# A block with attention and routed experts on one core: thirty-two more tokens by gathered rows, dense products on 352 columns

## The chip, the cores and the metric

One core of a Trainium2 chip runs the kernel. The metric is the device time of one execution in microseconds (us); the kernel before and the kernel after are compared by the medians of their runs.

## What is computed

The reference is one layer on 512 tokens of width 1024: a modulation vector from `c`, windowed attention and latent attention, a projection, and then a feed-forward of routed experts. The last part fills some three quarters of the time, and the change lies in it:

```python
def peer_ffn(h, w_query, sub_keys, u_table, v_table):
    q = (xt @ w_query).reshape(T, PEER_HEADS, 2, PEER_KEY_DIM // 2)
    s = jnp.einsum('thpd,hpnd->thpn', q, sub_keys)
    s_top, i_top = lax.top_k(s, K)                       # K = 16, 128 keys
    cand = (s_top[:, :, 0, :, None] + s_top[:, :, 1, None, :]).reshape(T, PEER_HEADS, K * K)
    best, bi = lax.top_k(cand, K)
    e = ...                                              # expert number, of 128 * 128
    g = jax.nn.softmax(best, axis=-1)
    a = gelu(einsum('tkd,td->tk', u_table[e], x))        # 8 heads * 16 = 128 experts a token
    y = einsum('tk,tkd->td', g * a, v_table[e])
```

Each token has 128 experts out of 16,384; `u_table` and `v_table` have 16,384 rows of 1024 floats each, 64 MB a table.

## The kernel before

The feed-forward has two ways to do the same thing. For three token blocks of 128 (384 tokens) it is dense: it computes the products with all 16,384 rows of `u`, tile by tile of 128 rows, takes the gelu, multiplies by a gate that is zero for experts that a token has not chosen, and multiplies by all of `v`. For the fourth block (128 tokens) it fetches the chosen rows: for each of the 128 slots (8 heads x 16) one indirect DMA gathers 128 rows of 4 KB, one for each token.

The first pass runs over the 128 tiles of `u` (line 1110). For tile n, SyncE loads 512 KB (`load_tile`, line 401), ScalarE rounds them to `hi` (line 723), GpSimd takes the rest `lo` (`low_u`, line 488), and TensorE does 24 matmuls of 384 columns (`dot`, lines 1085 to 1087). ScalarE's gelu (line 748) goes out to DRAM. `high(n + 2)` and so `low_u(n + 2)` wait for `dot(n - 1)`, so GpSimd is at most three tiles ahead.

Beside it VectorE searches the experts of a token block (`search`), in this order: block 0 of the search order is the gathered one (tiles 0 to 12), then three dense blocks, each with a search stretch of 18 tiles and a building stretch of 16 tiles, which begin at tiles 30, 64 and 98. In a building step, VectorE makes one-hot matrices for 8 tokens, ScalarE weighs them, and TensorE multiplies them into gates (`token_gates`, line 1096) after the dot of its tile. Gates of the first two dense blocks go to DRAM, those of the last stay in `stage`.

The rows are gathered by GpSimd in its one program order, between the `low_u` of the tiles (line 497). Five row buffers are used in turn: a gather waits until the buffer's last row was used (`row_used`), and a list written out ahead, `row_step`, holds it back to a tile. VectorE's `row_dot` (line 1443) multiplies a gathered row of `u` with the token (`x_tok`, in PSUM). There are 4 such rows in each search stretch and 2 or 3 in each building step. ScalarE's `weights(p)` is the exponential of a search; for block 0 it stands behind the gelu of tile 13. When all 128 are done (tile 115) ScalarE takes their gelu, and VectorE begins with the rows of `v` (`row_sum`, line 1543), 12 of them before the second pass.

The second pass runs over the 128 tiles of `v` (`mix`, lines 1132 to 1134, 24 matmuls of 384 columns for each tile). VectorE weighs the gelus that come back with the gates (`weigh`, lines 1521 and 1523), takes `lo` of the tile (`low_v`, line 1532) and of the weighed gelus (`low_c`, line 1527), and sums one more gathered row per tile. Sums are in y_tok, which is transposed to the output at the end (line 1150).

## Time and profile before

| | us |
|---|---|
| median of 3 runs | 1587.39 |
| lowest, highest | 1583.72, 1588.54 |
| profiled execution | 1583.69 |
| its span from first to last instruction | 1581.6 |

```profile
PE 1503.6 (95%) x8487; PEld 1392.4 (88%) x8487; DVE 1221.5 (77%) x2498; ACT 720.0 (46%) x1352; POOL 622.9 (39%) x414
```

PE is TensorE's matmuls, PEld its weight loads, DVE VectorE, ACT ScalarE, POOL GpSimd, SP SyncE. The numbers are busy time, its share of the span and instructions.

### The profile page before, as it was taken

To read this page: it belongs to the slowest core of one execution; us is meant where nothing else is said; L and a number is where in the kernel's file an instruction comes from. 1 tells how busy PE (TensorE), PEld (TensorE's weight loads), DVE (VectorE), ACT (ScalarE), POOL (GpSimd) and SP (SyncE) were. 2 spreads that over 40 slices of the span, in tenths; PEclk is the share of its full clock that TensorE was granted. 3 is DMA by queue.
4 is the path that set the end of the run, shared out by engine and by line. 5 is a ranking of instruction groups with operands and counts; after the bars stand their busy time and mean duration, and the time that the engine had idled before them with its cause. 6 is when DMAs were issued, how large, how long until landed. Compare 5 with 4: busy or idle time off the path is not lost.

```text
span 1581.6 us, 23400 instructions
## 1 busy us (share of the span) xinstructions
PE 1503.6 (95%) x8487; PEld 1392.4 (88%) x8487; DVE 1221.5 (77%) x2498; ACT 720.0 (46%) x1352; POOL 622.9 (39%) x414
## 2 busy tenths in 40 slices
PE   3898999989969999999999999999999999999998
PEld 3464566868969999999999999999999999999998
DVE  3857676865979688978899685778888888888874
ACT  1235465233323777357754777333333333333331
POOL 2001000201757777677777777932222222222200
PEclk9999579999989999999999999999999999999999
DMA  9820100443757699998999899899999999999973
GB/s 323 279 103 1 54 1 10 152 180 120 231 176 237 224 322 325 372 320 295 325 350 333 272 319 335 258 342 331 336 327 341 325 330 337 326 338 330 327 238 106
DMA packets 148369, 405.25 MB, mean 256 GB/s; under 512 B 15392, under 2 KB 49440, under 8 KB 147360
## 3 DMA queue, kind: packets, MB, share of 16 engines
q1 hardware_dynamic: 90816, 242.39, 45.5%
q0 software_dynamic: 36864, 134.23, 23.5%
q10 hardware_dynamic: 20576, 27.15, 4.7%
q8 instruction: 68, 1.11, 0.3%
q14 instruction: 45, 0.37, 0.1%
HBM read 356.53 MB, written 47.19 MB: 255 GB/s over the span
## 4 chain that ended last, share of the span: by engine, by line
PE 89%; DVE 3%; DMA 3%; ACT 2%; POOL 1%; issue 1%; SPq 0%; ACTq 0%; DVEq 0%
PE ps L1132 11%; PE ps L1134 11%; PE ps L1133 11%; PE ps L1085 10%; PE ps L1087 10%; PE ps L1086 10%; PE ps L1096 5%; PE ps L860 4%; PE ps L977 2%; PE ps L947 2%; PE ps L960 1%; PE ps L950 1%; DVE m L1178 1%; PE ps L1008 1%; DMA ring<-in_w_ada 1%
## 5 line engine op out<-in xcount | busy, mean ns | idle before, releaser
L723 ACT ACTIVATE hi<-raw 128x1024 fp32r<-128x1024 f32 x256 | 271.1, 1060 | 375.4 <-PE ps L1134 337.1
L488 POOL TENSOR_TENSOR lo<-raw,hi 128x1024 fp32r<-128x1024 f32 x128 | 327.4, 2560 | 194.0 <-ACT hi L723 190.6
L1085 PE MATMUL ps<-h2hi,hi 128*128 128x384 f32 x1024 | 347.9, 340 | 13.1 <-POOL lo L488 13.1
L1087 PE MATMUL ps<-h2hi,lo 128*128 128x384 f32 x1024 | 343.6, 336 | 0.0
L1086 PE MATMUL ps<-h2lo,hi 128*128 128x384 f32 x1024 | 343.3, 335 | 0.0
L1132 PE MATMUL ps<-chi,hi 128*128 128x384 f32 x1000 | 334.8, 335 | 3.2 <-DVE lo L1532 3.2
L1134 PE MATMUL ps<-chi,lo 128*128 128x384 f32 x1000 | 334.7, 335 | 0.0
L1133 PE MATMUL ps<-clo,hi 128*128 128x384 f32 x1000 | 334.6, 335 | 0.0
L1532 DVE TENSOR_TENSOR lo<-raw,hi 128x1024 fp32r<-128x1024 f32 x128 | 156.7, 1225 | 104.4 <-ACT hi L723 104.4
L1085 PEld LDWEIGHTS ps<-h2hi,hi 128*128 128x128 f32 x1024 | 193.2, 189 | 13.8 <-POOL lo L488 13.8
L1086 PEld LDWEIGHTS ps<-h2lo,hi 128*128 128x128 f32 x1024 | 193.2, 189 | 0.0
L1087 PEld LDWEIGHTS ps<-h2hi,lo 128*128 128x128 f32 x1024 | 192.9, 188 | 0.0
L1132 PEld LDWEIGHTS ps<-chi,hi 128*128 128x128 f32 x1000 | 188.3, 188 | 3.6 <-DVE lo L1532 3.6
L1133 PEld LDWEIGHTS ps<-clo,hi 128*128 128x128 f32 x1000 | 188.3, 188 | 0.0
L1134 PEld LDWEIGHTS ps<-chi,lo 128*128 128x128 f32 x1000 | 188.2, 188 | 0.0
L497 POOL DMA_INDIRECT rows<-in_v_tiles,E x76 | 80.5, 1059 | 219.4 <-DVE y_tok L1543 212.8
L748 ACT ACTIVATE act_out<-ps 128x384 f32<-128x384 f32 x128 | 62.3, 487 | 174.4 <-PE ps L1087 171.6
L759 ACT ACTIVATE ohW<-eqI,wS 128x128 f32<-128x128 f32 x384 | 118.2, 390 | 29.7 <-DVE eqI L1482 29.1
L1443 DVE SCALAR_TENSOR_TENSOR rows<-rows,ps 128x1024 f32<-128x1024 f32 x78 | 94.8, 1220 | 22.2 <-DMA rows<-in_u_rows,E 17.4
L1543 DVE SCALAR_TENSOR_TENSOR y_tok<-rows,cc,y_tok 128x1024 f32<-128x1024 f32 x76 | 107.0, 1407 | 4.7 <-DMA rows<-in_v_tiles,E 4.3
L1096 PE MATMUL ps<-ohW,ohJ 128*128 128x128 f32 x768 | 99.1, 278 | 5.4 <-issue 2.4
L1096 PEld LDWEIGHTS ps<-ohW,ohJ 128*128 128x128 f32 x768 | 93.1, 191 | 12.2 <-issue 7.6
(279 smaller groups left out, 2164.9 us busy)
## 6 DMA issues: line engine op xcount, KB each, us to landing
raw<-in_u_tiles SPq DMA_DIRECT2D x128, 512.0 KB
raw<-in_v_tiles SPq DMA_DIRECT2D x128, 512.0 KB
gelus<-act_out ACTq DMA_DIRECT2D x128, 192.0 KB
act_in<-gelus SPq DMA_DIRECT2D x128, 192.0 KB, 5.1
gates<-stage SPq DMA_DIRECT2D x32, 512.0 KB
gate<-gates SPq DMA_DIRECT2D x32, 512.0 KB
late<-in_w_ada SPq DMA_DIRECT2D x4, 2048.0 KB, 8.5
qkT<-in_w_ada SPq DMA_DIRECT2D x3, 2048.0 KB, 14.3
```

The source lines that it names most:

```text
L488: nc.gpsimd.tensor_tensor(lo[m % 3][:], raw[m % 3][:], hi[m % 3][:].bitcast(F32), ALU.subtract).then_inc(u_lo, 1)
L723: nc.scalar.activation(hi[m % 3][:], raw[m % 3][:], ACT.Copy).then_inc(t_hi, 1)
L759: last = nc.scalar.activation(ohW[half][:, t, :], eqI[:, half, t, :], ACT.Copy, scale=wS[:, col:col + 1])
L1085: nc.tensor.matmul(out, hi[n % 3][:, cols], h2hi[:, 0:ND, k, :], start=(k == 0), stop=False)
L1086: nc.tensor.matmul(out, hi[n % 3][:, cols], h2lo[:, 0:ND, k, :], start=False, stop=False)
L1087: last = nc.tensor.matmul(out, lo[n % 3][:, cols], h2hi[:, 0:ND, k, :], start=False, stop=(k == KD - 1))
L1096: last = nc.tensor.matmul(ps[:, 2 + half, t * P:(t + 1) * P], ohJ[half][:, t, :], ohW[half][:, t, :], start=True, stop=True)
L1132: nc.tensor.matmul(out, hi[m % 3][:, cols], chi[n % 4][:], start=(n == 0), stop=False)
L1133: nc.tensor.matmul(out, hi[m % 3][:, cols], clo[n % 4][:], start=False, stop=False)
L1134: last = nc.tensor.matmul(out, lo[m % 3][:, cols], chi[n % 4][:], start=False, stop=False)
L1532: tt_(lo[m % 3][:], raw[m % 3][:], hi[m % 3][:].bitcast(F32), ALU.subtract).then_inc(v_lo, 1)
L1543: nc.vector.scalar_tensor_tensor(out=y_tok[:], in0=row, scalar=cc[:, n:n + 1], in1=y_tok[:], op0=ALU.mult, op1=ALU.add).then_inc(row_used, 1)
```

## The change

32 tokens of the third dense block move from the dense way to the gathered one. The dense products have 352 columns instead of 384. The last building stretch has 12 steps instead of 16 and ends at tile 110 instead of 114. The 32 tokens' rows are gathered four slots at a time: one indirect DMA fetches 4 slots of each of 32 tokens, so that 32 more transfers suffice for `u` and 32 for `v`, 160 of each instead of 128.

`h2hi` and `h2lo`, the moving operand of `dot`, are laid out in groups of 32 tokens, so that 352 columns are 11 runs of 32, where 384 were 3 runs of 128. `x_tok` is made by 8 transposes at tile 4 (`turn_tokens`) from a sum that VectorE writes, instead of by 16 matmuls ahead of tile 0; at tile 111 it is made again for the 32 tokens, each four times. Their expert numbers and weights go to DRAM and back with four small DMAs on SyncE in the last building stretch. Their 32 `row_dot` follow from tile 112 on, three a tile by `row_step`; ScalarE's gelu of all the row products moves from tile 115 to tile 123, and the 12 early `row_sum` move behind it. In the second pass every sixth tile has two `row_sum`. At the end `y_more` is folded to 32 tokens by one matmul for each of 8 column groups.

In the search stretches 6 rows instead of 4 are used (1, 1, 2, 2). `weights(0)` moves from tile 13 to tile 10, and the first gather from GpSimd's tile 13 to tile 14.

```diff
-TD = ND * P
+XT = 32
+XR = P // XT
+TD = ND * P - XT
 SLOTS = PH * KTOP
+SU = SLOTS + SLOTS // XR
...
-        FILL, PER_BUILD, EARLY = 4, (2, 3), 12
+        steps_of = {p: BUILD if p < TT - 1 else BUILD - XT // (2 * HB) for p in range(1, TT)}
+        tail_at = build_at[TT - 1] + steps_of[TT - 1]
+        FILL, PER_BUILD, EARLY, MORE = (1, 1, 2, 2), (2, 3), 12, 6
...
-        row_step = row_step[:SLOTS] + [tail_at + 2 + j for j in range(EARLY)] + [NT + n for n in range(NT - EARLY)]
+        sums_at = [n for n in range(NT) for _ in range(2 if n % MORE == MORE - 1 else 1)][:SU - EARLY]
+        more_at = tail_at + 3 + (SU - SLOTS) // 3
+        row_step = row_step[:SLOTS] + [tail_at + 2 + j // 3 for j in range(SU - SLOTS)] + \
+            [more_at + 1 + j // 3 for j in range(EARLY)] + [NT + n for n in sums_at]
...
+                if m == build_at[TT - 1] + 6:
+                    sp.wait_ge(more_ready, 1)
+                    sp.dma_start(more[0], Ef[P - XT:P, :]).then_inc(more_out, 16)
+                    sp.dma_start(more[1], IJW[P - XT:P, 2, :, :].rearrange("p h k -> p (h k)")).then_inc(more_out, 16)
+                if m == build_at[TT - 1] + 8:
+                    sp.wait_ge(more_out, 32)
+                    sp.dma_start(E2[:].bitcast(F32), more[0].rearrange("t (r k) -> (t r) k", r=XR)).then_inc(more_in, 16)
+                    sp.dma_start(wg[:, SLOTS:SU], more[1].rearrange("t (r k) -> (t r) k", r=XR)).then_inc(more_in, 16)
...
-                while g < 2 * SLOTS and (row_step[g - NROWS] <= m - 3 if g >= NROWS else m >= S0 + 1):
+                while g < 2 * SU and (row_step[g - NROWS] <= m - 3 if g >= NROWS else m >= S0 + 2):
...
-                    if n == search_at[p] + (13 if p == 0 else 14):
+                    if n == search_at[p] + (10 if p == 0 else 14):
                         weights(p)
-                if n == tail_at + 1:
-                    act.wait_ge(row_used, SLOTS)
+                if n == more_at:
+                    act.wait_ge(row_used, SU)
                     nc.scalar.activation(cc[:], aa[:], ACT.Gelu).then_inc(aa_gelu, 1)
...
+            def turn_tokens(part, done):
+                pe.wait_ge(x_cols, done)
+                if done == 1:
+                    pe.wait_ge(s_copied, TT)
+                else:
+                    pe.wait_ge(row_used, SLOTS)
+                for k in range(KD):
+                    cols = slice(k * P, (k + 1) * P)
+                    last = nc.tensor.transpose(x_tok[:, cols], part[:, cols], ident[:])
+                last.then_inc(x_tok_ready, 1)
...
-                    nc.tensor.matmul(out, hi[n % 3][:, cols], h2hi[:, 0:ND, k, :], start=(k == 0), stop=False)
+                    nc.tensor.matmul(out, hi[n % 3][:, cols], dense(h2hi, k), start=(k == 0), stop=False)
...
+                if d == 0:
+                    pe.wait_ge(row_used, 2 * SU)
+                    pe.wait_ge(spread_ready, 1)
+                nc.tensor.transpose(ps[:, d, ND * P:T], y_tok[:, cols], ident[:])
+                nc.tensor.matmul(ps[:, d, TD:ND * P], y_more[:, cols], spread[:], start=True, stop=True).then_inc(y_ps, 1)
...
-                if n + EARLY < NT:
-                    row_sum(n + EARLY)
+                for j, at in enumerate(sums_at):
+                    if at == n:
+                        row_sum(EARLY + j)
```

## Rows read from the trace of the kernel before

**Rows 1.** The page's part on the chain that ended last, shares by engine.
```profile
PE 89%; DVE 3%; DMA 3%; ACT 2%; POOL 1%; issue 1%; SPq 0%; ACTq 0%; DVEq 0%
```

**Rows 2.** TensorE's waits from 400 us on: total us, times, longest us.
```profile
PE ps L1085 <- POOL lo L488: 13.1, 2, 12.9
PE ps L1132 <- DVE lo L1532: 3.2, 1, 3.2
```

**Rows 3.** Chain pieces (start, us, what): 32 matmuls of 512 columns, twice.
```profile
289.02 7.27 PE ps L1015 x32
...
344.44 7.25 PE ps L1015 x32
```

**Rows 4.** Windows: stretch, us, busy PE, PEld, DVE, ACT, POOL, PEclk, DMA, GB/s.
```profile
640.00:660.00 20.00, 20.00 (x117) 20.00 (x116) 19.72 (x89) 7.78 (x10) 13.13 (x6) 1.00 1.02 393
...
800.00:820.00 20.00, 19.62 (x117) 19.17 (x117) 19.80 (x99) 9.55 (x18) 14.52 (x10) 1.00 1.00 357
...
1040.00:1060.00 20.00, 19.72 (x105) 19.72 (x106) 15.56 (x25) 6.08 (x9) 4.58 (x4) 0.91 1.00 367
...
1200.00:1400.00 200.00, 200.00 (x1156) 200.00 (x1155) 164.83 (x242) 70.72 (x97) 49.76 (x49) 1.00 0.96 332
```

**Rows 5.** DMA queues (packets, MB, share) and issues (count, KB, us to landing).
```profile
q0 software_dynamic: 36864, 134.23, 23.5%
...
raw<-in_v_tiles SPq DMA_DIRECT2D x128, 512.0 KB
...
act_in<-gelus SPq DMA_DIRECT2D x128, 192.0 KB, 5.1
...
gate<-gates SPq DMA_DIRECT2D x32, 512.0 KB
```

**Rows 6.** Timeline 440 to 467 us (start, us, what), of DVE, POOL and PE.
```profile
449.31 0.29 DVE L1473 TENSOR_REDUCE eS<-eW 128x8 f32<-128x128 f32 x1 [8.35 <-ACT eW L770]
...
451.03 1.12 POOL L497 DMA_INDIRECT rows<-in_u_rows,E  x1 [10.13 <-DVE E L1490]
...
466.10 0.33 PE L1085 MATMUL ps<-h2hi,hi 128*128 128x384 f32 x1
```

**Rows 7.** Chain pieces in building: token gates; a loop from hi to gates.
```profile
533.18 1.78 PE ps L1096 x16
539.14 1.78 PE ps L1096 x16
...
626.99 1.78 PE ps L1096 x16
...
728.38 1.06 ACT hi L723
...
734.57 7.99 DMA rows<-in_u_rows,E
...
745.82 1.13 PE ps L1096 x8
```

**Rows 8.** Timeline of POOL in a building step with three gathers.
```profile
955.92 2.40 POOL L488 TENSOR_TENSOR lo<-raw,hi 128x1024 fp32r<-128x1024 f32 x1 [1.23 <-ACT hi L723]
...
962.13 2.41 POOL L488 TENSOR_TENSOR lo<-raw,hi 128x1024 fp32r<-128x1024 f32 x1 [0.22 <-ACT hi L723]
```

**Rows 9.** Timeline: DVE's second search begins and ends; PE turns its result.
```profile
630.41 2.80 DVE L1423 MAX8 sv<-s 128x8 f32<-128x128 f32 x14
...
694.38 0.51 DVE L1476 TENSOR_TENSOR IJW<-eW,eR 128x128 f32<-128x128 f32 x1
...
703.51 0.49 PE L1103 MATMUL ps<-ident,IJW 128*128 128x128 f32 x3
```

**Rows 10.** Timeline of DVE: a row sum beside low_u, one without.
```profile
1012.08 2.96 DVE L1543 SCALAR_TENSOR_TENSOR y_tok<-rows,cc,y_tok 128x1024 f32<-128x1024 f32 x1 [1.39 <-DMA rows<-in_v_tiles,E]
...
1056.94 1.28 DVE L1543 SCALAR_TENSOR_TENSOR y_tok<-row_hi,cc,y_tok 128x1024 f32<-128x1024 f32 x1
```

**Rows 11.** Timeline of PE: the last three tiles of the second pass begin.
```profile
1564.60 0.44 PE L1146 MATMUL ps<-chi,hi 128*128 128x384 f32 x1 [2.46 <-DVE lo L1532]
```

More of the change, by code:

```diff
@@ L163, in build @@
         (row_lo,), _ = region(at2 + (TT + ND) * KD * P * 4, [("row_lo", [P, D], F32)])
+        x_part = rows[0]
         rows = [t[:] for t in rows + [row_hi, row_lo]]
@@ L369, in group, with dense, gathered, gathered_more @@
             return (p - 1) * 2 * BUILD + 2 * i + half
-        NGROUPS = ND * 2 * BUILD
+        NGROUPS = 2 * sum(steps_of.values())
+        def dense(of, k):
+            return of[:, 0:TD // XT, k, :]
+        def gathered(of):
+            return of[:, ND * P // XT:T // XT, :, :]
+        def gathered_more(of):
+            return of[:, TD // XT, :, :].unsqueeze(3).to_broadcast([P, KD, XT, XR])
         block = ctx.enter_context(nc.Block())
@@ L1067, in _ @@
                 key_scores(tt)
-            pe.wait_ge(h2_split, KD)
             pe.wait_ge(s_copied, TT - 1)
-            pe.wait_ge(identr_ready, 1)
-            for k in range(KD):
-                out = x_tok[:, k * P:(k + 1) * P]
-                nc.tensor.matmul(out, h2hi[:, TT - 1, k, :], identr[:], start=True, stop=False)
-                last = nc.tensor.matmul(out, h2lo[:, TT - 1, k, :], identr[:], start=False, stop=True)
-            last.then_inc(x_tok_ready, 1)
+            def turn_tokens(part, done):
[8 more added lines that the diff above has]
+                last.then_inc(x_tok_ready, 1)
             def dot(n):
@@ L1084, in dot @@
                     cols = slice(k * P, (k + 1) * P)
-                    nc.tensor.matmul(out, hi[n % 3][:, cols], h2hi[:, 0:ND, k, :], start=(k == 0), stop=False)
-                    nc.tensor.matmul(out, hi[n % 3][:, cols], h2lo[:, 0:ND, k, :], start=False, stop=False)
-                    last = nc.tensor.matmul(out, lo[n % 3][:, cols], h2hi[:, 0:ND, k, :], start=False, stop=(k == KD - 1))
+                    nc.tensor.matmul(out, hi[n % 3][:, cols], dense(h2hi, k), start=(k == 0), stop=False)
+                    nc.tensor.matmul(out, hi[n % 3][:, cols], dense(h2lo, k), start=False, stop=False)
+                    last = nc.tensor.matmul(out, lo[n % 3][:, cols], dense(h2hi, k), start=False, stop=(k == KD - 1))
                 last.then_inc(a_ps, 1)
@@ L1418, in _, with top16 @@
             dve.sem_inc(ada_read, 1)
-            def top16(vals, idx, lists, n, between):
+            def top16(vals, idx, lists, n, between, fills):
                 for a in range(n):
@@ L1427, in top16 @@
                 settled(last)
-                between()
+                between(fills[0])
                 for a in range(n):
@@ L1434, in top16 @@
                 settled(last)
-                between()
+                between(fills[1])
                 for a in range(n):
@@ L1534, in row_sum @@
             def row_sum(n):
-                g = SLOTS + n
+                g = SU + n
                 dve.wait_ge(row_in[g % NROWS], 16 * (g // NROWS + 1))
                 dve.wait_ge(cc_ready, 1)
-                row = rows[g % NROWS]
-                if n == 0:
-                    nc.vector.tensor_scalar(y_tok[:], row, cc[:, n:n + 1], None, ALU.mult).then_inc(row_used, 1)
+                if n == SLOTS:
+                    dve.wait_ge(a_ps, NT)
+                row, y = rows[g % NROWS], y_tok if n < SLOTS else y_more
+                if n in (0, SLOTS):
+                    nc.vector.tensor_scalar(y[:], row, cc[:, n:n + 1], None, ALU.mult).then_inc(row_used, 1)
                 else:
                     dve.wait_ge(row_used, g)
-                    nc.vector.scalar_tensor_tensor(out=y_tok[:], in0=row, scalar=cc[:, n:n + 1], in1=y_tok[:],
+                    nc.vector.scalar_tensor_tensor(out=y[:], in0=row, scalar=cc[:, n:n + 1], in1=y[:],
                                                    op0=ALU.mult, op1=ALU.add).then_inc(row_used, 1)
+            dve.wait_ge(oh_used, NGROUPS + 2)
+            tt_(y_tok[:].rearrange("p (k t r) -> p k t r", k=KD, r=XR), gathered_more(h2hi).bitcast(F32), gathered_more(h2lo).bitcast(F32), ALU.add)\
+                .then_inc(x_cols, 1)
+            for g in range(SLOTS, SU):
+                row_dot(g)
             dve.wait_ge(aa_gelu, 1)
+            dve.wait_ge(more_in, 32)
             tt_(cc[:], cc[:], wg[:], ALU.mult).then_inc(cc_ready, 1)
```

89 lines of the change are left out of this document (54 added, 35 removed).

## Prediction

> **What bounds the kernel now.** I read the chain of work that ended last first: 89% of it is TensorE [rows 1]. Then TensorE's own waits from 400 us on, to see whether something else is nearly late: in some 1180 us they are one stop of 12.9 us behind GpSimd and one of 3.2 us at the start of the second pass, and little else [rows 2]. Then the windows of the second pass: TensorE is busy for all of 200 us, while the DMA engines are busy for 0.96 of it and move 332 GB/s [rows 4]. So the kernel is bound by matmul columns, with the transfers close behind. The change removes columns and adds transfers; all depends on what is late next.
>
> **What a tile costs.** In the second pass 1156 matmuls of 384 columns start in 200 us [rows 4], 173.0 ns each, so 24 of them take 4.15 us. 32 matmuls of 512 columns take 7.27 us, 227 ns each [rows 3]. The difference is 0.42 ns a column, one column a cycle of the full clock. 352 columns then take 159.5 ns and a tile 3.83 us, 0.32 us less. The new moving operand of `dot` comes in 11 runs of 32 columns. No row has such runs; the nearest is the second of the two pieces, whose operand `h2hi` comes in 4 runs of 128 and which takes 7.25 us, where the first, contiguous one takes 7.27 [rows 3]. I take nothing for it, and price it as a rival.
>
> I now follow the first pass from landmark to landmark, in the times of the profiled span.
>
> **Start to tile 15.** Now VectorE waits 8.35 us for the exponential behind tile 13's gelu, ending at 449.31; the expert numbers follow 1.7 us later, GpSimd stands at the first gather for 10.13 us, does five and only then the next `low_u`; `dot(15)` starts at 466.10 [rows 6]. With the exponential at tile 10 VectorE finds it done, so the numbers are ready at 442.7. GpSimd is then through `low_u(14)`. A gather takes it 1.2 us ((6.0 - 2.4) / 3) [rows 8], five 6.1, and `low_u(15)` 2.4, so `dot(15)` can start at 451.5. By columns it would be ready a little earlier: without the stop of 12.9 us it would be at 453 now, some 4 us less with shorter tiles, and the 8 transposes at tile 4 add 0.7 (three start 0.25 us ahead of the dot that follows, so 0.08 each) [rows 9]. So 451.5 is the start, 14.6 us earlier.
>
> **Tiles 15 to 30.** 15 x 3.83 = 57.5 us give 509.0. VectorE's search now begins at 443 and took 64.5 us in the second block (630.41 to 694.89) [rows 9]. Two more row products of 1.3 us make 67.1, and the first rows, which are gathered at 443 to 449, may keep it waiting: I take 70, bounds 67 and 72. TensorE waits for it, where in the second block it comes 8.6 us after (694.89 to 703.51) [rows 9]. Start of building: 513.
>
> **Building stretches.** A step costs 5.96 us when nothing waits (533.18 to 539.14), but 15 steps take 93.8 us, 6.25 each [rows 7]. The difference is a loop: after one step's gates ScalarE rounds, GpSimd subtracts and gathers, the rows land 7 to 8 us after issue, VectorE uses them and only then makes the one-hots; 728.38 to 745.82 is 17.4 us of it [rows 7], and it spans three steps. Shorter dots don't shorten this loop. The floor becomes 5.64; bounds are 5.64 and 6.25, and I take 6.05, since most stalled steps will be set by the loop as before. 16 steps: 96.8 us, twice; the last stretch has 12: 72.6.
>
> **Search stretches two and three.** 18 x 3.83 + 0.3 = 69.2 us. VectorE starts 1.6 us after the first of these dots (630.41 against 626.99 + 1.78) [rows 7, 9] and needs 64.5 + 2.6: done at 68.7. So 69.7 each, with no slack left. The small DMAs on SyncE at tiles 104 and 106 wait for things that are long done and sit ahead of loads that have two tiles of lead: nothing.
>
> Sum: 513 + 96.8 = 609.8; + 69.7 = 679.5; + 96.8 = 776.3; + 69.7 = 846.0; + 72.6 = 918.6 at the end of the building.
>
> **Tiles 110 to 127.** TensorE alone needs 18 x 3.83 + 0.7 = 69.6 us. But from GpSimd's tile 115 on there are three gathers behind each `low_u`. In a building step that had three, `low_u` to the next possible one took 6.0 us (955.92 to 962.13 less 0.22 of waiting) [rows 8]. A tile's transfers are 0.52 + 0.18 MB and three gathers of 0.524 (134.23 MB over 256) [rows 5], 2.28 MB; at 6.0 us that is 380 GB/s, about as much as the fullest window shows (393) [rows 4]. I take 6.15. `low_u(115)` ends 15.8 us into this part; ten such tiles later `low_u(125)` ends at 77.3, `low_u(127)` at 84.9, and `dot(127)` at 90.0. That is 20 us behind the columns.
>
> **The turn to the second pass.** ScalarE's gelu of the row products needs the 160th row: gathered in tile 123, used at 76. The rows of `v` that five buffers hold come along, but the other seven gathers are issued behind `low_u(127)`. A landing takes between the 5.1 us of the loads of `act_in` and the 8.0 of a gather in the building [rows 5, 7]; I take the lower, since the burst is short. With 1.2 us to issue, 1.3 a sum and five buffers, that is some 1.6 us each: the twelfth is summed at 103, and `low_v(0)` follows at 106.2, as VectorE takes it after all twelve. TensorE waits 16 us, where it now waits 3.2 [rows 2]. `low_v(0)`, and `load_tile` behind it on SyncE, wait for the same. Row sums took 2.96 us beside a `low_u` and 1.28 without one [rows 10]; only the first few fall beside it. Bounds 99 and 116. The page SBUF — State Buffer of the Trainium skill (its part on the two sides of SBUF and their shared port pair) says that a VectorE operation with two SBUF inputs and a GpSimd operation exclude each other; the 2.96 us agree. Second pass starts at 918.6 + 106.2 = 1024.8.
>
> **The second pass.** Bytes of a tile: 0.524 + 0.197 + 0.131 + 0.524 = 1.376 MB now [rows 5], which at 4.15 us are the 332 GB/s read [rows 4]. After it is 0.524 + 0.180 + 0.131 + 148/127 x 0.524 = 1.446 MB, and 3.83 us would ask for 377 GB/s. The window in which this pass catches up moved 367, and windows in the first pass 357 and 393 [rows 4]. VectorE is busy 164.83 of 200 us, 3.42 a tile, and comes to 3.56 with 0.165 sums more and 0.05 less of columns: below 3.83, and a tile with two sums (4.7) is covered by the two tiles that it is ahead. I take 3.90, a little over the columns. 125 x 3.90 = 487.5 us. The clock falls once after the wait, as it does now (0.91 over 20 us) [rows 4]: 1.7 us. Then the 2.46 us stop and the end, 17.0 us from 1564.60 [rows 11]; two more row sums lie behind the last `low_v` now and TensorE waits for them at the first column group: 2.8 us. The fold matmuls (0.1 us each) eat what the columns save there.
>
> 1024.8 + 1.7 + 487.5 + 2.5 + 2.8 + 17.0 = 1536.3 us of span against 1581.6. The profiled execution took 1583.69, 2.1 more than its span, so 1538.4; the median of the runs is 3.7 above it, so 1542.
>
> The page DMA: Bandwidth & Descriptors of the Trainium skill (part Bandwidth) gives some 358 GB/s as what HBM yields to a core, which speaks against this change; but 393 GB/s over 20 us [rows 4] is more. It is the first rival below.
>
> **Rivals.**
> 1. The transfers set the second pass. If a backlog moves no more than the 357 GB/s of 800 to 820 us, at a DMA share of 1.00 [rows 4], a tile takes 1.446 / 0.357 = 4.05 us: 19 us more, and 2 in tiles 115 to 125: 1563. For it: DMA share 0.96 already. Against: the 393. The same with the waiting in each transfer kept as it is (0.96 x 1.446/1.376 of 4.15 us): 4.18 us, 1577. The page's limit would give nearly the 4.05.
> 2. The turn is worse: row landings of 8.0 us and sums of 2.96 us [rows 7, 10], or a clock at half while TensorE idles 2.3 of each 6.15 us (a tile then takes up to 7.7): 15 to 25 us more, 1562.
> 3. Slower: a run of 32 columns costs something at each join. There are 10 joins x 24 x 128. From 2.4 ns a join (6 columns) a dot is 0.58 us longer and the gain is gone (74 plain tiles x 0.58, and 44 building tiles past the loop's slack). At 4 ns: 74 x 0.96 + 44 x 0.55 = 95 us, 1637. Against it: no cost for runs of 128 [rows 3]; for it, no row this short.
> 4. The columns don't count, since weight loads bound a matmul: tile stays 4.15, +10 to 40 us, about 1585. Against it: 512 and 384 columns differ by a cycle for each column, so at 384 the columns set the time [rows 3, 4].
>
> **How the numbers follow.** Forecast 0.47 (1522 to 1556); rival 1 0.20 at 1563 and 0.08 at 1577; rival 2 0.13; rival 4 or mixtures near no change 0.04; rival 3, with any mixture of 1 and 2 that overshoots, 0.08. The range 1522 to 1578 takes the bounds of the building step (5.75 to 6.25: -13 to +9 us), of the turn (-7 to +10) and of the second pass (3.83 to 4.16: -9 to +33). Faster by over 0.3% 0.88, within 0.3% (about what a measurement of this kernel can tell) 0.04, slower 0.08.
>
> **What would show it.** `dot(15)` near 451; plain tiles at 3.83; building steps near 6.05; `low_u` 6.1 us apart at tiles 115 to 125 with TensorE waiting for it; a stop of some 16 us ahead of line 1132's counterpart for `low_v`; second pass tiles at 3.90 with TensorE mostly busy. It is wrong if tiles of the second pass stand at 4.0 or more with ScalarE's `hi` waiting for DMA, or if plain dots are longer than their columns.

## The result and the profile after

The changed kernel takes 1571.6 us (median of 6 runs, 1570.1 to 1577.3) against 1584.8 us (6 runs). The ratio is 0.991, with a 95% interval of 0.989 to 0.993: some 13 us less. One execution each of e2_one_run and e9_half_rows took far longer than the others of its kernel (4207.9 and 2785.5 us) and is left out of the figures below. The forecast was 1542. The sign was right, and two thirds of the gain did not come. The profiled execution took 1575.6 us with a span of 1573.1; the working had 1536.3 for it, so 36.8 us of span have to be found.

The page, its part on busy time of the changed kernel:

```profile
PE 1449.0 (92%) x8439; PEld 1332.0 (85%) x8439; DVE 1265.0 (80%) x2583; ACT 706.4 (45%) x1311; POOL 768.1 (49%) x478
```

TensorE works 54.6 us less than before, and the span is only 8.5 us shorter: 46 us have become waiting. TensorE's waits from 400 us on, changed kernel (us in total, times, longest), to be held against [rows 2]:

```profile
PE ps L1123 <- POOL lo L519: 24.8, 15, 3.0
PE ps L1134 <- DVE ohJ L1531: 21.2, 9, 5.0
PE ps L1174 <- DVE lo L1588: 16.9, 1, 16.9
PE ps L1188 <- DVE lo L1588: 2.5, 1, 2.5
```

Before there was one stop of 12.9 us behind GpSimd. Now 15 tiles wait for GpSimd's low part, nine building steps wait for VectorE's one-hots, and the turn waits 16.9 us.

Windows of the changed kernel (columns as in [rows 4]): the second pass, a search stretch, and the tail of the first pass.

```profile
1100.00:1300.00 200.00, 200.00 (x1259) 200.00 (x1258) 184.75 (x273) 79.69 (x106) 103.62 (x62) 1.00 1.01 379
...
820.00:860.00 40.00, 40.00 (x245) 40.00 (x245) 39.51 (x163) 15.26 (x20) 27.76 (x14) 1.00 1.01 377
...
980.00:1000.00 20.00, 16.27 (x87) 15.38 (x86) 8.86 (x15) 6.10 (x8) 17.21 (x15) 0.91 0.94 343
1000.00:1020.00 20.00, 14.67 (x78) 13.79 (x77) 12.48 (x21) 4.57 (x6) 17.33 (x15) 0.92 1.01 389
```

In the second pass TensorE is busy throughout, 200 / 1259 = 158.9 ns a matmul (forecast 159.5), while the DMA engines move 379 GB/s. In the search stretch it is also busy throughout, but a matmul takes 40 / 245 = 163.3 ns. In the tail the DMA engines are full and TensorE is not.

Where the time stands, from the starts of the dots in the two traces and the forecast (us; a stretch is from the start of one dot to that of the other, and `mix(0)` is the start of the second pass):

| stretch | before | forecast | after |
|---|---|---|---|
| start to dot(15) | 466.1 | 451.5 | 457.8 |
| dot(15) to dot(30) | 62.6 | 61.5 | 64.0 |
| building, dot(30) to dot(46) | 99.8 | 96.8 | 105.2 |
| search, dot(46) to dot(64) | 75.2 | 69.7 | 75.4 |
| building, dot(64) to dot(80) | 100.5 | 96.8 | 106.4 |
| search, dot(80) to dot(98) | 75.2 | 69.7 | 73.2 |
| building, dot(98) to dot(110) | 74.5 | 72.6 | 77.6 |
| tail and turn, dot(110) to mix(0) | 86.3 | 106.2 | 111.3 |
| mix(0) to the end | 541.3 | 511.5 | 502.2 |

The second pass gave more than was forecast. Every stretch of the first pass is longer than forecast, and the building stretches, with fewer columns, are longer than before.

The largest single stop is in the third step of each building stretch. The chain of work through the first of them, changed kernel (start, us, what):

```profile
528.28 1.06 ACT hi L757
529.35 0.07 issue
529.41 2.41 POOL lo L519
531.83 0.14 issue
531.97 7.12 DMA rows<-in_u_rows,E
539.09 0.02 issue
539.11 1.23 DVE rows L1490 x2
540.34 0.60 DVE eqI L1529
540.94 0.61 DVE ohJ L1531
541.55 0.80 issue
542.35 3.67 PE ps L1134 x16
```

`low_u(33)` has to be done before a gather is issued at 531.97. Its row lands 7.12 us later, and only then does VectorE make the one-hots for the gates of tile 32. `dot(33)` starts 12.50 us after `dot(32)` where 5.73 is the step. At tiles 67 and 101 the pitches are 12.40 and 10.99.

### The profile page after: what moved, and what is told of

It is laid out like the page before. It is cut to its first block, busy times and chain, and to the rows that moved or that the text cites. A ratio compares the mean times of both kernels' runs of the same rounds, so it can differ in the third digit from the quotient of the medians.

```text
span 1573.1 us, 23445 instructions
## 1 busy us (share of the span) xinstructions
PE 1449.0 (92%) x8439; PEld 1332.0 (85%) x8439; DVE 1265.0 (80%) x2583; ACT 706.4 (45%) x1311; POOL 768.1 (49%) x478
## 4 chain that ended last, share of the span: by engine, by line
PE 66%; DVE 10%; POOL 9%; DMA 8%; ACT 3%; issue 3%; ACTq 0%; SPq 0%; DVEq 0%
PE ps L1174 10%; PE ps L1175 10%; PE ps L1176 10%; POOL lo L519 6%; DMA rows<-in_u_rows,E 5%; PE ps L1123 5%; PE ps L1125 4%; PE ps L1124 4%; PE ps L893 4%; PE ps L1134 2%; PE ps L1010 2%; POOL rows L531 2%; PE ps L980 2%; PE ps L993 1%; PE ps L983 1%
## 5 line engine op out<-in xcount | busy, mean ns | idle before, releaser
L1123 PE MATMUL ps<-h2hi,hi 128*128 128x352 f32 x1024 | 346.7, 339 | 25.8 <-POOL lo L519 24.8
L1125 PE MATMUL ps<-h2hi,lo 128*128 128x352 f32 x1024 | 340.1, 332 | 0.0
L1174 PE MATMUL ps<-chi,hi 128*128 128x352 f32 x1000 | 322.6, 323 | 16.9 <-DVE lo L1588 16.9
L1124 PE MATMUL ps<-h2lo,hi 128*128 128x352 f32 x1024 | 337.9, 330 | 0.0
L1175 PE MATMUL ps<-clo,hi 128*128 128x352 f32 x1000 | 322.3, 322 | 0.0
L1176 PE MATMUL ps<-chi,lo 128*128 128x352 f32 x1000 | 322.3, 322 | 0.0
L531 POOL DMA_INDIRECT rows<-in_v_tiles,E x96 | 153.3, 1597 | 151.2 <-DVE y_tok L1601 121.4
L1490 DVE SCALAR_TENSOR_TENSOR rows<-rows,ps 128x1024 f32<-128x1024 f32 x96 | 116.0, 1219 | 54.3 <-DMA rows<-in_u_rows,E 53.0
L781 ACT ACTIVATE act_out<-ps 128x352 f32<-128x352 f32 x128 | 58.9, 460 | 172.2 <-PE ps L1125 163.6
L792 ACT ACTIVATE ohW<-eqI,wS 128x128 f32<-128x128 f32 x352 | 108.2, 390 | 40.9 <-DVE eqI L1529 40.8
L1134 PE MATMUL ps<-ohW,ohJ 128*128 128x128 f32 x704 | 95.6, 289 | 24.3 <-DVE ohJ L1531 21.2
```

Source lines behind the costliest of these rows:

```text
L531: nc.gpsimd.indirect_dma_start(rows[g % NROWS], None, table, bass.IndirectOffsetOnAxis(ap=at, axis=0)).then_inc(row_in[g % NROWS], 16)
L1123: nc.tensor.matmul(out, hi[n % 3][:, cols], dense(h2hi, k), start=(k == 0), stop=False)
L1124: nc.tensor.matmul(out, hi[n % 3][:, cols], dense(h2lo, k), start=False, stop=False)
L1125: last = nc.tensor.matmul(out, lo[n % 3][:, cols], dense(h2hi, k), start=False, stop=(k == KD - 1))
L1134: last = nc.tensor.matmul(ps[:, 2 + half, t * P:(t + 1) * P], ohJ[half][:, t, :], ohW[half][:, t, :], start=True, stop=True)
L1174: nc.tensor.matmul(out, hi[m % 3][:, cols], chi[n % 4][:], start=(n == 0), stop=False)
```

## The experiments

All edits are to the changed kernel, but for `e3_exp_alone`. Six kernels compute other numbers than the reference (e2_one_run, e8_both_one_run, e9_half_rows, e10_half_rows_vector, e13_half_low_start, e14_half_low_search): they are for their times alone. Ratios are to the kernel before in the same group of runs, with their 95% interval; 0.001 is 1.6 us. The changed kernel has 0.991.

**The held gathers (e1_rows_early).**

```diff
-            row_step += [search_at[p] + 3 * (j + 1) for j in range(sum(FILL))]
+            row_step += [search_at[p] + at for at in (3, 6, 9, 11, 13, 15)]
```

> The six rows of a search stretch are given to tiles 3, 6, 9, 11, 13 and 15 of the stretch in the list that holds gathers back, instead of 3, 6, 9, 12, 15 and 18; nothing else changes. Theory A: the list holds the third row of the second building step back to GpSimd's tile build_at + 3, and that makes the stop of some 6.5 us in the third step of each building stretch (pitches 12.50, 12.40 and 10.99 us at tiles 33, 67 and 101). Then those three pitches fall to 6 to 7.5 us and the kernel is 14 to 19 us faster than the changed kernel, 1553 to 1558. Theory B: the landing of 7 us and the loop of the building steps make the stop, wherever the gather stands; it then moves to a neighbouring step, and the kernel gains less than 4 us, 1568 or more.

1552.1 us, ratio 0.979 (0.977 to 0.980): 19.5 us less than the changed kernel. All three pitches are 5.73. GpSimd's timeline at the place, e1_rows_early:

```profile
528.08 2.41 POOL L519 TENSOR_TENSOR lo<-raw,hi 128x1024 fp32r<-128x1024 f32 x1 [3.21 <-ACT hi L757]
530.63 0.95 POOL L531 DMA_INDIRECT rows<-in_u_rows,E  x1
531.89 0.94 POOL L531 DMA_INDIRECT rows<-in_u_rows,E  x1 [0.30 <-issue]
```

Two gathers stand there, where the changed kernel has three:

```profile
529.41 2.41 POOL L519 TENSOR_TENSOR lo<-raw,hi 128x1024 fp32r<-128x1024 f32 x1 [3.22 <-ACT hi L757]
531.97 0.95 POOL L531 DMA_INDIRECT rows<-in_u_rows,E  x1
533.23 0.94 POOL L531 DMA_INDIRECT rows<-in_u_rows,E  x1 [0.30 <-issue]
534.47 0.94 POOL L531 DMA_INDIRECT rows<-in_u_rows,E  x1 [0.30 <-issue]
```

The first of the three is for the fifth row of the stretch, which the second step uses. `row_step` gave the sixth search row to tile 18 of the stretch, the first of the building, so the gather five rows on was held with those of the building. The three building stretches lose 4.4, 6.4 and 3.7 us, 14.5 of the 18.0 us of span; the rest is the small balance of the start, the search stretches (one of which is 1.5 us longer) and the tail. Theory A holds, and the pitches fell further than it had them (6 to 7.5).

**The joins (e2_one_run).**

```diff
-            return of[:, 0:TD // XT, k, :]
+            return of[:].rearrange("p g k c -> p (g k c)")[:, k * TD:(k + 1) * TD]
```

> The moving operand of dot is read as one run of 352 columns from the same buffers, which holds other tokens' and other features' numbers, so the dense products of the first pass are of other data; the count of matmuls and columns is the same. Theory A: the 10 joins of each matmul cost 5.4 ns (pitch 3.95 us a plain tile in the first pass, 3.82 in the second, where the operand is one run). Then plain tiles of the first pass stand at 3.82 to 3.84 us; some 66 of them are bound by TensorE, which gives 8 us, and the building steps give 0 to 4: 1560 to 1564. Theory B: the 0.13 us a tile comes from something else that the first pass has (weights that GpSimd and ScalarE write meanwhile); the pitch stays at 3.95 and the time within 2 us of the changed kernel.

The pitches are close to theory A: plain tiles at 3.81 us (tiles 20 to 26) and 3.87 us (tiles 48 to 55 and 82 to 89) instead of 3.95, building steps at 5.60 at least instead of 5.73. So the joins cost 0.08 to 0.14 us a tile, 3.3 to 5.6 ns a matmul. The same window as above, e2_one_run:

```profile
820.00:860.00 40.00, 40.00 (x250) 40.00 (x249) 39.44 (x138) 16.17 (x22) 30.98 (x14) 1.00 0.99 372
```

In this window it is 160.0 ns a matmul instead of 163.3. The time does not follow: 1577.3 us, ratio 0.995 (0.993 to 0.997), which is above the changed kernel, though the profiled execution's span is 5.5 us shorter. TensorE waits longer for GpSimd (31.2 us against 24.8) and for the one-hots (24.3 against 21.2). So the cost of a join is shown, and its worth in the whole kernel is not: there is only the 5.5 us between two single executions, and that of the changed kernel (1575.6 us) lies 4 us above its median. Why the other runs were slower is open.

**The exponential and the first gather alone (e3_exp_alone), on the kernel before.**

```diff
-                    if n == search_at[p] + (13 if p == 0 else 14):
+                    if n == search_at[p] + (10 if p == 0 else 14):
...
-                while g < 2 * SLOTS and (row_step[g - NROWS] <= m - 3 if g >= NROWS else m >= S0 + 1):
+                while g < 2 * SLOTS and (row_step[g - NROWS] <= m - 3 if g >= NROWS else m >= S0 + 2):
```

> The kernel before with one part of the change alone: the first exponential behind the gelu of tile 10 instead of 13 and the first gather behind GpSimd's tile 14 instead of 13. Theory A (the forecast's step): the stop of 12.9 us ahead of dot 15 goes, and nothing else is late until the first building stretch, so the kernel is 10 to 13 us faster than before, 1572 to 1575. Theory B: the search of the second token block or a stop at tiles 15 to 30 takes most of it back, as in the changed kernel, where dot 30 comes only 6.9 us earlier than before: 3 to 7 us, 1578 to 1582.

1572.1 us, ratio 0.993 (0.990 to 0.996), 13.3 us less than before. TensorE's waits for GpSimd, e3_exp_alone:

```profile
PE ps L1085 <- POOL lo L488: 2.4, 2, 2.2
```

The stop of 12.9 us is gone and nothing takes its place. This two-line part alone is worth as much as the whole change.

**The other part alone (e12_tokens_alone).** Both edits of e3 taken back in the changed kernel.

```diff
-                    if n == search_at[p] + (10 if p == 0 else 14):
+                    if n == search_at[p] + (13 if p == 0 else 14):
...
-                while g < 2 * SU and (row_step[g - NROWS] <= m - 3 if g >= NROWS else m >= S0 + 2):
+                while g < 2 * SU and (row_step[g - NROWS] <= m - 3 if g >= NROWS else m >= S0 + 1):
```

> The changed kernel without the move of the first exponential and of the first gather: the exponential stands behind the gelu of tile 13 again, the first gather behind GpSimd's tile 13. So it is the 32 tokens' part of the change with the six rows a search stretch. Theory A: the parts add. The move alone gave 13.3 us (e3_exp_alone) and the whole change 13.2, so that the tokens' part gives nothing by itself: 1582 to 1588. Theory B: in the changed kernel part of the move's gain is lost again at tiles 15 to 30, so undoing it costs less, 5 to 10 us: 1576 to 1581.

1580.4 us, ratio 0.997 (0.995 to 0.999): theory B, by a little. The 32 tokens as they were written bring 2 to 8 us; the move is worth 9 us within the changed kernel. As theory B has it, part of the move's gain goes again at tiles 15 to 30, which take 64.0 us in the changed kernel and 59.4 here. Its trace again has

```profile
PE ps L1123 <- POOL lo L519: 18.5, 2, 12.9
```

from 400 to 520 us.

**The turn (e4_five_early).**

```diff
-        FILL, PER_BUILD, EARLY, MORE = (1, 1, 2, 2), (2, 3), 12, 6
+        FILL, PER_BUILD, EARLY, MORE = (1, 1, 2, 2), (2, 3), 5, 4
```

> 5 row sums instead of 12 ahead of the second pass, and two sums in every fourth tile of it instead of every sixth. Theory A: TensorE's wait of 16.9 us at the turn is for the seven gathers behind low_u(127) and their sums, so that it falls to 5 to 9 us and the kernel is 8 to 12 us faster than the changed kernel, 1560 to 1564. Theory B: the wait passes to another (the gelu of the row products, or the gelus that come back), or VectorE, busy 185 of 200 us in the second pass, becomes its bound with 7 more sums: 0 to 3 us, 1569 or more.

1561.4 us, ratio 0.984 (0.982 to 0.986), 10.2 us less than the changed kernel. Of the wait ahead of `mix(0)`, e4_five_early:

```profile
PE ps L1174 <- DVE lo L1588: 3.5, 1, 3.5
```

is left. The second pass stays at 3.84 us a tile with seven more sums in it. Theory A.

**Both (e6_both).** The edits of e1_rows_early and e4_five_early.

> e1_rows_early and e4_five_early together. Theory A: the stops in the building and the wait at the turn are separate, so the gains add: 1571.6 less 19.5 less 10.2 is 1542, range 1539 to 1545. Theory B: one hides the other (the wait at the turn is met by whatever is late next once the tail begins sooner), 1547 to 1552.

1540.0 us, ratio 0.970 (0.967 to 0.973). 0.991 less 0.012 and 0.007 is 0.972: they add. All that follows builds on it, but for e5_rows_at_use, which builds on e1_rows_early.

**The joins once more (e8_both_one_run).** The edits of e6_both and of e2_one_run.

> e6_both with the moving operand of dot read as one run of 352 columns (other data, as in e2_one_run, so the dense products are of other numbers). e2_one_run had plain tiles at 3.81 to 3.87 us and building steps at 5.60 at least, against 3.95 and 5.73, yet its median was 5.7 us above that of the changed kernel, with TensorE's waits for GpSimd and VectorE longer. Theory A: the joins cost what the pitches say and the waits had eaten it; with the longest stops gone 5 to 10 us are left, 1532 to 1537. Theory B: the stretches are bound by GpSimd, VectorE and the rows, and not by the columns, so the shorter dots give nothing: within 3 us of e6_both, or slower with a lower granted clock.

Ratio 0.968 (0.966 to 0.971) against 0.970; the span is 8.9 us shorter (1531.2 against 1540.1), the median of the runs 4.0. The interval does not part this from nothing, so that the two theories stay open as to the time, though the median of 1536.1 us lies where theory A had it. The building stretches take 99.7, 98.3 and 73.3 us against 100.8, 99.6 and 74.8, the search stretches 72.5 and 71.0 against 77.2 and 72.3.

**What sets the tail (e7_vector_low, e9_half_rows, e10_half_rows_vector).** e7_vector_low gives six low parts to VectorE, e9_half_rows halves the bytes of the 32 gathers, e10_half_rows_vector does both.

```diff
+        by_vector = (114, 116, 118, 120, 122, 124)
...
+            for m in by_vector:
+                while g < SU and row_step[g] + 3 <= m:
+                    row_dot(g)
+                    g += 1
+                dve.wait_ge(u_lo, m)
+                dve.wait_ge(t_hi, m + 1)
+                tt_(lo[m % 3][:], raw[m % 3][:], hi[m % 3][:].bitcast(F32), ALU.subtract).then_inc(u_lo, 1)
```

```diff
+                out = rows[g % NROWS]
+                if SLOTS <= g < SU:
+                    out, table = out[:, 0:D // 2], table.rearrange("n (a d) -> (n a) d", a=2)
```

> e6_both, and VectorE takes the low parts of tiles 114, 116, 118, 120, 122 and 124 of the first pass (1.2 us each there) instead of GpSimd (2.4 us each). Theory A: GpSimd's program, 2.40 + 3 x 1.25 us a tile, sets the 6.0 us between the low parts at tiles 115 to 125. Then two tiles take it 2.4 + 6 x 1.25 = 9.9 us, a tile 4.95, and the kernel is 8 to 12 us faster than e6_both, 1530 to 1534. Theory B: the five row buffers set it, each with a gather's issue, a landing of 5 to 8 us and a row product of 1.3: 1.8 to 2.0 us a row, 5.4 to 6.0 a tile; then the gain is under 4 us and VectorE waits for rows meanwhile.

> e6_both, with the 32 gathers for the row products of the 32 tokens fetching 2 KB a row instead of 4 KB (from a table seen as 32768 rows of 512, so those products are of other numbers; count of instructions unchanged). In e6_both the low parts of tiles 117 to 124 are 6.0 us apart, GpSimd's program is 2.40 + 3 x 1.25, and the DMA engines are at a share of 1.00 with 375 GB/s: both fit. e7_vector_low took half of the low parts from GpSimd and dot 110 to dot 127 stayed at 89.3 us (88.6 in e6_both). Theory A: the transfers set the pace alone; then with 0.26 MB instead of 0.52 a row the pitch of tiles 117 to 124 falls to 3.95 to 5 us and the kernel is 8 to 16 us faster than e6_both, 1524 to 1532. Theory B: GpSimd's program is as long as the transfers, so one hides behind the other: the pitch stays at 6.0 and the time within 3 us of e6_both, 1537 to 1543.

> e7_vector_low with the same 32 gathers of 2 KB a row. Theory A and theory B of e9_half_rows both make this one faster than e7_vector_low, since neither GpSimd nor the transfers fill 6.0 us a tile: two tiles take GpSimd 9.9 us, so dot 110 to dot 127 falls from 89.3 to 72 to 78 us and the time to 1522 to 1530. Under B this is the only one of e7_vector_low, e9_half_rows and this one that gains in the tail. Theory C: the landing of a row and five buffers set it (a landing of 5 to 8 us hardly depends on the bytes): then the tail stays at 85 us or more.

Ratios 0.968 (0.965 to 0.971), 0.970 (0.966 to 0.974) and 0.966 (0.964 to 0.967). From `dot(110)` to `dot(127)`: 89.3, 88.1 and 82.0 us, against 88.6 in e6_both. So neither edit moves the tail, and both together do. Windows (DVE, ACT, POOL are the third to fifth busy times), e7_vector_low:

```profile
980.00:1000.00 20.00, 14.77 (x80) 14.48 (x81) 14.60 (x23) 4.21 (x7) 15.54 (x12) 0.91 1.01 383
```

e9_half_rows:

```profile
980.00:1000.00 20.00, 16.06 (x86) 15.18 (x85) 11.93 (x21) 4.57 (x6) 17.16 (x14) 0.91 0.76 258
```

With GpSimd relieved the transfers are full at 383 GB/s. With the transfers relieved (258 GB/s) GpSimd is as busy as before and its low parts stay 6.0 us apart. This is theory B of e9_half_rows: GpSimd's program alone gives 6.0 us for a tile with three rows, and with GpSimd relieved the fetching of the rows gives about the same (two tiles 11.6 to 12.4 us apart in e7_vector_low). Whether there it is the rate of 383 GB/s or the round trip of five buffers isn't parted, since half the bytes can shorten both. With both edits two tiles are 9.8 to 11.1 us apart, and the 82.0 us are above the 72 to 78 expected; VectorE still waits for landings there, which bears on theory C in part. The 3 us that e7_vector_low's median lies below e6_both are not from the tail.

**Where VectorE and GpSimd meet (e5_rows_at_use, e13_half_low_start, e14_half_low_search).** In e1_rows_early the search stretch from tile 46 took 76.9 us and `dot(64)` came 9.70 us after `dot(63)`. VectorE's timeline there, e1_rows_early:

```profile
691.74 0.29 DVE L1520 TENSOR_REDUCE eS<-eW 128x8 f32<-128x128 f32 x1
692.06 0.20 DVE L1521 RECIPROCAL eR<-eS 128x8 f32<-128x8 f32 x1
692.30 5.27 DVE L1523 TENSOR_TENSOR IJW<-eW,eR 128x128 f32<-128x128 f32 x1
```

and GpSimd's:

```profile
687.57 4.07 POOL L519 TENSOR_TENSOR lo<-raw,hi 128x1024 fp32r<-128x1024 f32 x1 [0.33 <-ACT hi L757]
691.79 0.96 POOL L531 DMA_INDIRECT rows<-in_u_rows,E  x1 [0.15 <-issue]
692.76 4.65 POOL L519 TENSOR_TENSOR lo<-raw,hi 128x1024 fp32r<-128x1024 f32 x2
```

An operation on 128 elements ends at 697.57 us, when the second of GpSimd's two low parts is done (697.41). The first edit takes the gathers out of that place, the second and third let GpSimd compute half of its columns in some tiles:

```diff
-            row_step += [search_at[p] + 3 * (j + 1) for j in range(sum(FILL))]
+            row_step += [search_at[p] + at for at in (3, 5, 9, 9, 11, 11)]
```

```diff
+                n = D // 2 if 26 <= m <= 31 or 59 <= m <= 66 or 93 <= m <= 100 else D
-                nc.gpsimd.tensor_tensor(lo[m % 3][:], raw[m % 3][:], hi[m % 3][:].bitcast(F32), ALU.subtract).then_inc(u_lo, 1)
+                nc.gpsimd.tensor_tensor(lo[m % 3][:, 0:n], raw[m % 3][:, 0:n], hi[m % 3][:, 0:n].bitcast(F32), ALU.subtract).then_inc(u_lo, 1)
```

(`3 <= m <= 14` in e13_half_low_start.)

> As e1_rows_early, but the six rows of a search stretch are given to the tiles at which VectorE uses them, 3, 5, 9, 9, 11 and 11 of the stretch, so that no gather of a search stretch stands behind GpSimd's tiles 61 to 66 or 95 to 100. Those tiles lie beside VectorE's comparisons with two operands in SBUF, where in e1_rows_early a VectorE operation of 128x128 took 5.27 us behind low_u, gather, low_u, low_u, the search ended at 697.6 and dot 64 came 9.70 us after dot 63. Theory A: VectorE and GpSimd hold each other up there, by whole operations, so that fewer GpSimd operations free VectorE: the search of the third token block ends 3 to 6 us sooner in its stretch and the pitch at tile 64 falls to 4 to 6.5 us; the kernel takes 1546 to 1550. Theory B: VectorE waits for rows, or the search is as long whatever GpSimd does; then the time is within 2 us of e1_rows_early.

> e6_both, where GpSimd computes the low parts of tiles 26 to 31, 59 to 66 and 93 to 100 for 512 of 1024 columns (those dense products lack a correction). Theory A: the two engines hold each other up at the end of each search. Then dot 46 to dot 64 takes 71 to 72 us and dot 80 to dot 98 too (77.2 and 72.3 in e6_both; the columns alone are 71.1 and a little for the gates of the last step), no pitch at tiles 60 to 64 is above 4.3, and the time is 1533 to 1537. Theory B: the search waits for rows or for its own chain: dot 46 to dot 64 stays between 72.5 and 77.5 and the time at 1540.

> e6_both, where GpSimd computes the low parts of tiles 3 to 14 for 512 of 1024 columns (the other half is left as it was, so those dense products lack a correction). Theory A: one GpSimd operation of 2.4 us that becomes 3.6 to 4.4 us beside VectorE's operations with two operands in SBUF makes the stop at tiles 3 and 4 (dot 5 comes 29.8 to 35.3 us after the first rounding of a tile, the late ones where low part 3 took 3.6 us or more), and the same makes the first search longer. Then dot 5 comes 28 to 30 us after the first rounding, dot 30 comes 2 to 5 us sooner than e6_both's 137.4 after it, and the time is 1535 to 1539. Theory B: the late load of tile 3 makes the stop; dot 5 stays where it was, at 34 to 35 with a late load, and the time at 1540.

e5_rows_at_use: 1556.1 us, ratio 0.982 (0.979 to 0.984), no better than e1_rows_early's 0.979. The stretch took 73.8 us and the pitch at tile 64 was 5.92, but kernels with e1's rows have it between 72.3 and 77.7, so this run decides nothing, and the expected 1546 to 1550 was wrong.

e14_half_low_search: ratio 0.965 (0.962 to 0.967) against 0.970, both search stretches at 71.4 us (77.2 and 72.3), no pitch above 4.2 at tiles 58 to 64. The same operation there, e14_half_low_search:

```profile
683.32 0.29 DVE L1524 TENSOR_TENSOR IJW<-eW,eR 128x128 f32<-128x128 f32 x1
```

0.29 us, where e1_rows_early has 5.27 and e6_both, on which this kernel builds, 1.77. In e6_both it is GpSimd that comes late: `dot(59)` to `dot(62)` wait for its low parts, with pitches of 4.40, 6.93 and 5.45 us. Its timeline with VectorE's beside it, e6_both:

```profile
669.90 8.73 POOL L519 TENSOR_TENSOR lo<-raw,hi 128x1024 fp32r<-128x1024 f32 x2 [2.58 <-ACT hi L757]
681.87 6.01 POOL L519 TENSOR_TENSOR lo<-raw,hi 128x1024 fp32r<-128x1024 f32 x2
```

```profile
669.70 2.29 DVE L1515 TENSOR_TENSOR cand<-abf,iota 128x2048 f32<-128x2048 f32 x1
672.03 4.34 DVE L1517 TENSOR_TENSOR cand<-cand,sixf 128x2048 f32<-128x2048 f32 x1
681.05 2.29 DVE L1517 TENSOR_TENSOR cand<-cand,sixf 128x2048 f32<-128x2048 f32 x1
```

Two low parts take 8.73 us where one alone takes 2.40, and VectorE's line 1517 takes 4.34 us or 2.29. Theory A. The edit also takes half of its own work from GpSimd, and how much of the 5.8 us of the first stretch is this isn't parted. The page SBUF — State Buffer of the Trainium skill (its part on the two sides of SBUF and their shared port pair) says that a VectorE operation with two SBUF inputs and a GpSimd operation that reads SBUF exclude each other; these traces agree.

e13_half_low_start: ratio 0.965 (0.962 to 0.969). `dot(5)` comes 28.7 us after the first rounding of a tile, where the kernels with the full operation have 28.5 to 29.8 or 34.2 to 35.5 (31.3 in the changed kernel, 32.5 in e2_one_run), and `dot(30)` 129.9 us after it instead of 137.5. Tile 3's load came early in this run as well (17.4 us after the first rounding, 19 in the late ones), so what made `dot(5)` early can't be told from it. Against the kernels of 352 columns in which `dot(5)` came as early (28.5 to 29.8 us) and `dot(30)` 134.0 to 136.5 us after the first rounding, `dot(30)` comes 4.1 to 6.6 us sooner, and this speaks for theory A. The median, 1531.3 us, is below the 1535 to 1539 expected.

**Three early sums (e11_three_early) and two rows a tile (e15_two_a_tile).**

```diff
-        FILL, PER_BUILD, EARLY, MORE = (1, 1, 2, 2), (2, 3), 5, 4
+        FILL, PER_BUILD, EARLY, MORE = (1, 1, 2, 2), (2, 3), 3, 4
...
-                    if n == 4:
+                    if n == 9:
                         turn_tokens(x_part, 1)
```

> e6_both with 3 early row sums instead of 5 (157 in the second pass, two in every fourth tile), and the eight transposes of the gathered tokens ahead of dot 9 instead of dot 4. Theory A: the wait of 3.5 us at the turn loses 2 us more, and the transposes, which stand now where TensorE's granted clock is at half behind the wait for tile 3, cost 0.7 us instead of 0.9 to 2.8: 1 to 3 us less than e6_both in the ratio to before, 0.968 to 0.970. Theory B: the turn is then set by the gelus and the low parts, the start by the load of tile 3, and nothing changes: 0.970 to 0.972.

Ratio 0.968 (0.966 to 0.970): 0.002 below e6_both, which the intervals don't part. The turn waits 3.1 us instead of 3.5.

```diff
-        more_at = tail_at + 3 + (SU - SLOTS) // 3
-        row_step = row_step[:SLOTS] + [tail_at + 2 + j // 3 for j in range(SU - SLOTS)] + \
+        more_at = NT - 1
+        row_step = row_step[:SLOTS] + [tail_at + 2 + j // 2 for j in range(SU - SLOTS)] + \
...
+            for n in range(3):
+                weigh(n)
+                low_c(n)
+                if n < 2:
+                    low_v(n)
             dve.wait_ge(aa_gelu, 1)
...
             for n in range(EARLY):
                 row_sum(n)
-                if n >= EARLY - 3:
-                    weigh(n - (EARLY - 3))
-                    low_c(n - (EARLY - 3))
-            low_v(0)
-            low_v(1)
```

> e11_three_early, but the 32 row products of the 32 tokens go two to a tile (tiles 112 to 127) instead of three, the gelu of the row products stands behind tile 127 instead of 123, and VectorE takes the first three weighings and the first two low parts of the second pass ahead of the three early sums. Theory A: three rows a tile fill GpSimd (2.40 + 3 x 1.25) and the transfers (375 to 389 GB/s) to 6.0 us, two need 4.9 us and 1.75 MB. Then dot 110 to dot 127 falls from 89.2 to 78 to 82 us, the wait at the turn stays below 8 us since the sums are out of its way, and the ratio to before is 0.962 to 0.966. Theory B: what the tail gains the turn loses, as the last products and their sums then lie behind dot 127: the second pass starts 95 us or more after dot 110, as in e11_three_early (96.5), and the ratio is 0.967 to 0.970.

1533.3 us, ratio 0.965 (0.962 to 0.967), the best kernel of this study that computes all. `dot(110)` to `dot(127)` takes 76.3 us instead of 89.2, the second pass starts 90.8 us after `dot(110)` instead of 96.5: more than half of what the tail gains goes to the turn (waits of 11.2 us, where theory A had less than 8). The ratio is where theory A had it. The tail and then the second pass, e15_two_a_tile:

```profile
980.00:1000.00 20.00, 17.77 (x104) 16.59 (x103) 10.59 (x19) 6.10 (x8) 18.07 (x13) 1.00 1.00 373
1000.00:1020.00 20.00, 17.59 (x101) 16.11 (x99) 10.43 (x17) 3.52 (x5) 17.49 (x14) 1.00 0.98 364
1100.00:1300.00 200.00, 200.00 (x1259) 200.00 (x1258) 190.23 (x278) 80.39 (x105) 131.36 (x67) 1.00 1.02 393
```

The granted clock stays at 1.00 in the tail, where it was at 0.91 and 0.92 with the stops of three rows a tile. The low parts are 4.8 us apart.

## Why the prediction was right and wrong

**What a tile costs.** In the second pass right to 0.6 ns a matmul. In the first pass the step "I take nothing for it", said of the runs of 32, was wrong: 3.95 against 3.82 us a tile in the second pass, 5.4 ns a matmul, 0.5 ns for each of 10 joins; read as one run in the first pass itself (e2_one_run) it is 3.3 to 5.6 ns. The query products show it too. They were left out of the sum: 32 matmuls of 512 columns take now

```profile
347.40 7.57 PE ps L1048 x32
```

against 7.25 in [rows 3], 0.32 / 32 = 10 ns for 12 more joins, and the products from the first `h2hi` to the last `qpT` take 50.2 us instead of 48.1. Runs of 128 had been no evidence for runs of 32. Rival 3's mechanism is real at some fifth of the 2.4 ns that it needed.

**Start to tile 15.** 6.3 us late. 4 of them stand already at the first rounding of a tile (383.9 against 379.8): 2.1 are the joins in the query products; the rest lies ahead of these, and the kernels with this part unchanged have that rounding anywhere from 380.5 to 383.9. The stop behind the exponential went as forecast, and e3_exp_alone shows its full worth.

**Tiles 15 to 30.** 2.5 us over the forecast, of which 15 x 0.12 = 1.8 are the joins.

**Building stretches.** The term of 6.05 us a step was a little low but within its bounds for all steps but one: without the third step 15 steps take 92.7 us, 6.18 each. The failed step is "I take 6.05, since most stalled steps will be set by the loop as before": the two more rows of a search were priced on VectorE alone ("Two more row products of 1.3 us"), and not in `row_step`, which decides when the gathers five rows on may start. That held one gather and cost 14.5 us in the three stretches, 19.5 us in the whole (e1_rows_early). It is the largest part of what the forecast missed: 18.0 of 36.8 us of span.

**Search stretches.** 5.7 and 3.5 us longer than forecast: the joins are 18 x 0.12 = 2.2 us of each, the rest went with half of GpSimd's work in e14_half_low_search (71.4 us), where the traces show GpSimd and VectorE holding each other up. "So 69.7 each, with no slack left" named the place and not this cause.

**Tiles 110 to 127.** The low parts are 6.0 us apart (6.15 forecast), but the row of them begins late: `low_u(115)` ends 20.4 us after the start of `dot(110)`, forecast 15.8, and `low_u(127)` at 88.4, forecast 84.9. The forecast's 90.0 is the end of `dot(127)` (20 us behind the 69.6 of the columns); it starts at 90.2 and ends at 94.3. These 4 us are most of the 5.0 us by which the second pass starts late; what made `low_u(115)` late was not tested. The same 6.0 us come about when GpSimd is relieved (e7_vector_low), at 383 GB/s: the forecast had worked out both limits, 380 GB/s among them, and went by GpSimd's. Spread to two rows a tile, the tail loses 12.9 us and the turn takes 7.2 of them back (e15_two_a_tile).

**The turn.** TensorE waits 16.9 us, forecast 16; e4_five_early confirms that seven gathers and sums made it. Rival 2 did not happen: the wait is 0.9 us over the forecast, and the granted clock in the tail was 0.91 and 0.92.

**The second pass.** Forecast 3.90 us a tile, measured 3.835 from `mix(0)` to `mix(124)`: 8 us of the 9.3 that this part is short of the sum. TensorE's wait for `y_more` at the first column group was 1.0 us, forecast 2.8. Rival 4 falls with the pitch of 3.84 us. Rival 1 is refuted: 379 GB/s here and 393 GB/s in e15_two_a_tile over 200 us, without TensorE waiting. The page DMA: Bandwidth & Descriptors of the Trainium skill (part Bandwidth) has some 358 GB/s for a core, but the same part gives that as a core's share when both cores of a memory stream, and has 425 GB/s for a core by itself. The prediction took only the first figure. Here one core ran the kernel, and the measured 393 GB/s is above the one and below the other.

So the mechanism (columns for transfers) held: `mix(0)` to `mix(124)` fell from 517.5 to 475.6 us, 42 us, more than the forecast had. What failed is the first pass down to `dot(110)`, 41 us over its forecast by the table: one entry of a list, the joins, and an engine pair with no room left; the tail and the turn added 5 us, and the second pass gave 9 back. 19.5 us of time came back with the six numbers of e1_rows_early. The median lies above the 1522 to 1556 given for the forecast itself; that it is inside the wider range, to 1578, is luck, since most of that width was for a slow second pass, and the second pass was faster than forecast.

## What to carry to other kernels

When a list written out by hand decides when a transfer may start, run the new list against the old one entry by entry around each boundary: an entry that moves across one holds back the transfer that comes as many places later as there are buffers. When work is moved from one engine to the transfers, price the engine that issues them and the transfers separately: two limits that are equal hide each other, and relieving one shows nothing. A cost that was measured for an operand in long runs is no evidence for one in short runs.

## What the runs showed of the hardware

A moving operand in 11 runs of 32 columns costs 3.3 to 5.6 ns a matmul over one run of 352 (3.95 us for 24 matmuls in the changed kernel, 3.81 and 3.87 in e2_one_run); 3 runs of 128 cost nothing that shows (4.16 us a tile of 384 columns in both passes before). A 128x128 operation of VectorE took 5.27 us (e1_rows_early) instead of 0.29 (e14_half_low_search), across two GpSimd operations in a row, while GpSimd's 2.40 became 3.6 to 4.5. The core sustained 393 GB/s over 200 us beside a TensorE that was never idle (e15_two_a_tile). The search stretch from tile 46 took 72.3 us in e10_half_rows_vector and 77.2 us in e6_both, whose programs differ only in the tail of the first pass; what decides which of the two a kernel gets is open.
